# Six of sixteen modulation chunks multiplied and summed on VectorE, with TensorE adding the two sums over the partitions

## The chip, the cores and the metric

The kernel runs on one core of a Trainium2 chip. The metric is the device time of one execution, in microseconds. The kernel before took 989.61 us, the median of three runs (989.29, 989.61 and 990.34).

Five engines work side by side, each through its own instruction list in order, and meet only at semaphores: TensorE (PE) multiplies matrices, VectorE (DVE) and ScalarE (ACT) work elementwise, GpSimd (POOL) and SyncE (SP) mostly start DMA transfers here.

## The reference, cut to what matters

One layer of a diffusion backbone: an adaLN modulation, a bidirectional mLSTM, a pooling branch, a mixture of experts, a final norm. The change touches only the modulation, which is computed for two conditioning vectors, one for the 128 context tokens and one for the 512 latent tokens:

```python
mod_ctx = jax.nn.silu(c_ctx)[None, :] @ w_mod[l] + b_mod[l]      # (1, 6 * 1024)
mod_lat = jax.nn.silu(c) @ w_mod[l] + b_mod[l]                   # (1, 6 * 1024)
shift1, scale1, gate1, shift2, scale2, gate2 = [m[:, None, :] for m in jnp.split(mod, 6, axis=-1)]
h = _rmsnorm(x, g_norm1) * (1 + scale1) + shift1
proj = h @ w_in + b_in            # q, k, v, o, gates, pooling columns, branch gates
...
x = x + gate1 * (merged @ w_out)
h2 = _rmsnorm(x, g_norm2) * (1 + scale2) + shift2
```

`w_mod` is 1024 x 6144 in float32. The first 2048 columns (shift1, scale1) are needed before the input projection can start. The other 4096 (gate1, shift2, scale2, gate2) are needed much later.

## The kernel before, in words

**Weights come in chunks of 1 MB** (128 partitions x 2048 floats), from one array in the order of use, into four buffers `raw0` to `raw3`. SP's loop (line 411) takes chunk c into buffer c % 4 (in the stretch that matters here), and only when chunk c - 4 has been released (`raw_free`). It does so strictly in order: a chunk whose buffer is not free holds up all later ones.

**The stretch of the change** is the q/k projection, `for j in range(1, N_QK)` (line 1842), and the first value blocks behind it (line 1878). In step j, TensorE does two blocks of q or k columns (`block_q`, 48 matmuls of 128x320 each) and two modulation products (`mod2_product`, 2j-2 and 2j-1). Numbered as in SP's loop, the chunks are:

| step | q/k chunk multiplied | modulation chunks used (numbers 2j-2, 2j-1) | chunk split for the step after |
|---|---|---|---|
| j = 5 | 21 | 22, 23 (numbers 8, 9) | 24 |
| j = 6 | 24 | 25, 26 (10, 11) | 27 |
| j = 7 | 27 | 28, 29 (12, 13) | 30, the first value chunk |
| values | 30, 33, 34, 35 | 31, 32 (14, 15), behind the first value block | 33, 34, 35 |

**The split.** A float32 weight chunk that TensorE multiplies is first split in a high part (ScalarE, `split_hi`, line 631) and a low part (VectorE, `split_lo`, line 1024); three matmuls then make one product. `split_lo` releases the raw buffer. In step j, ScalarE waits until TensorE has finished step j-1, and for the chunk to have landed; VectorE's low part follows; TensorE needs both at step j+1.

**The modulation products** of the second part need no split. For 1024 = 8 x 128 rows and two halves of 2048 columns there are 16 chunks. `mod2_product` (line 1746) multiplies 128 rows of the 2048 columns by the 32-column tile `csil` (its first two columns are the two silu vectors, the rest is zero) in four matmuls, one for each 32-column strip of the array, and adds up eight chunks in PSUM bank 6. It releases the raw buffer. Once chunk 15 is in, ScalarE copies bank 6 (`mod_row2`, line 682), TensorE turns the row into columns (`mod2_turned`, line 1834), VectorE adds the bias (`mod_add`, line 1086), and TensorE transposes the result once more (line 1888). VectorE has little other work in steps 5 to 7: one `split_lo` each, and a small `mod_add(0)` in step 5.

**Value blocks.** `value_block(c, t)` (line 1853) is 12 matmuls of 128x512, for c = 0 to 3 and five token tiles t. Products 14 and 15 stand behind block (0, 0). Later on, PSUM results go to `Vt` with a bias. On GpSimd the ones column of `Vt` is set at the very start (line 477), and the first broadcast of the maxima (`load_maxima(0)`, line 484) waits for ScalarE's two row stores.

Of the kernel before, what the change touches and what calls it, by code (L numbers as in the profile page):

```python
# [16 lines left out]
ALU = mybir.AluOpType  # L17
# [3 lines left out]
P = 128  # L21
D = 1024
KT = D // P
# [14 lines left out]
CH = 2048  # L38
# [17 lines left out]
N_QK, N_MOD2, N_V, N_O, N_U, N_G, N_B, N_A, N_OUT = 8, 16, 4, 4, 2, 8, 2, 4, 4  # L56
# [6 lines left out]
AT_A = AT_B + N_B  # L63
AT_OUT = AT_A + N_A
N_DENSE = AT_OUT + N_OUT


C_ID, C_ONE, C_FWD, C_BWD, C_STRICT, C_IOTA, C_NEGF, C_NEGB = (P * i for i in range(8))
# [52 lines left out]
def qk_at(j):  # L121
    return AT_QK + 3 * (j - 1) if j else 0


def m2_at(g):
    return AT_QK + 1 + 3 * g if g < N_QK - 1 else AT_V - 1


def m2_chunk(i):
    return m2_at(i // 2) + i % 2  # L130


def v_at(i):
    return AT_V + i if i else AT_V - 2


def raw_slot(c):
    return (c - AT_O) % 2 if AT_O <= c < AT_G + 4 else c % NRAW


def raw_use(c):
    return sum(raw_slot(b) == raw_slot(c) for b in range(c))


def raw_uses(s):
    return sum(raw_slot(b) == s for b in range(N_DENSE))

# [5 lines left out]
def gate_up_at(p):  # L153
    return ECH * p - 2 if p else 0
# [6 lines left out]
def layer_kernel(nc, x_d, small_d, wst_d, wg_d, wpool_d, st_d, rcnt_d,  # L161
                 wexp_d, xt_d, gf_d, bv_d, y_d, so_d, mo_d):
    ctx = ExitStack()
    with ctx:
# [3 lines left out]
        def at(name, kib, shape, dt=F32):  # L168
            return nc.alloc_sbuf_tensor_at(name, shape, dt, offset=base + int(kib * 1024))

        def sem(name):
            return ctx.enter_context(nc.semaphore(name))
# [30 lines left out]
        raw = [at(f"raw{s}", 8 + 8 * s, [P, CH]) for s in range(NRAW)]  # L203
# [4 lines left out]
        hn = at("hn", 112, [P, KT, T])  # L208
# [12 lines left out]
        negM = at("negM", TMP + 22.5, [R16, T])  # L221

        QH, QL = whi, wlo
        csil = at("csil", 176.75, [P, KT, 32])
        vb = at("vb", 178.5, [P, D])
        mst = at("mst", 183, [P, 4, 2, KT])
# [92 lines left out]
        ps = ctx.enter_context(nc.psum_tensor("ps", [P, 8, 512], F32))  # L319
# [8 lines left out]
        def f32(t):  # L328
# [10 lines left out]
        raw_full = [sem(f"raw_full{s}") for s in range(NRAW)]  # L339
        raw_free = [sem(f"raw_free{s}") for s in range(NRAW)]  # L340
        hi_ready = sem("hi_ready")
        blk_ready, pair_free = sem("blk_ready"), [sem(f"pair_free{s}") for s in range(4)]
        o_hi, o_lo, s_sqh = sem("o_hi"), sem("o_lo"), sem("s_sqh")
        s_csil, s_sq, s_ssq, s_rstd, s_hn, s_hhi, s_hlo = (sem(n) for n in (
            "s_csil", "s_sq", "s_ssq", "s_rstd", "s_hn", "s_hhi", "s_hlo"))
        d_wg, s_gain = sem("d_wg"), sem("s_gain")
        s_wgh, s_wgl, s_gps, s_gate, s_lsg, s_grow, s_gtok = (sem(n) for n in (
            "s_wgh", "s_wgl", "s_gps", "s_gate", "s_lsg", "s_grow", "s_gtok"))
# [1 line left out]
        d_vb, d_rows = sem("d_vb"), sem("d_rows")  # L350
# [19 lines left out]
        f_a, f_b, f_c, f_y, f_sq, f_rs, f_out, s_out, s_sum1 = (sem(n) for n in (  # L370
            "f_a", "f_b", "f_c", "f_y", "f_sq", "f_rs", "f_out", "s_out", "s_sum1"))
# [11 lines left out]
        def chunk_used(eng, c):  # L383
            eng.wait_ge(raw_free[raw_slot(c)], raw_use(c) + 2)
# [88 lines left out]
        def _(gp):  # L473
            st = Steps(gp, g_steps)
            gp.memset(gOne[:, :], 1.0).then_inc(s_init, 1)

            gp.memset(Vt[:, :, :, DH:V1], 1.0).then_inc(s_init, 1)
            gp.wait_ge(d_rows, 32)
            chunk_used(gp, m2_at(N_QK - 1) + 1)

            def load_maxima(h):
                if h >= 2:
# [28 lines left out]
            for g, w in enumerate(WIN):  # L511
# [7 lines left out]
                n, s, src = GW + 2 * PAD, 1, 0  # L519
# [14 lines left out]
                else:  # L534
                    st.do(gp.tensor_copy(RP[0][:, w // 2:w // 2 + GR, :], xs))
                    n, s, src = GR + w - 1, 1, 0
# [13 lines left out]
                n, s, src = TC + 2 * PAD, 1, 0  # L550
# [71 lines left out]
        def _(act):  # L622
# [3 lines left out]
            st = Steps(act, a_steps)  # L626
# [18 lines left out]
            act.activation(wgh[:, :, :], wgr[:, :, :], ACT.Copy).then_inc(s_wgh, 1)  # L645
            act.preload_act_table_set(LN_EXP)
            split_hi(0, QH[0])
            act.wait_ge(s_ssq, 1)
            inv_rms(halves(rstd[:, :]), ps[:, 0:2, 0:HALF], D, s_rstd)
            for i in range(4):  # L650
                chunk_used(act, AT_M1 + 2 * i + 1)
# [28 lines left out]
                   .then_inc(q_free, 1)  # L680

            def mod_row2(i):
                chunk_used(act, m2_chunk(KT * i + KT - 1))
                if i:
                    act.wait_ge(s_modT, i + 4)
                act.activation(mrow[:, :], ps[:, 6, :], ACT.Copy).then_inc(s_mrow, 1)
# [141 lines left out]
            for j in range(N_G):  # L828
# [3 lines left out]
                for b in range(2):  # L832
                    f = 2 * j + b
# [10 lines left out]
            for j in range(N_A + 2):  # L844
                c = AT_A + j
# [76 lines left out]
            with act.Fori(0, last_round) as r:  # L922
# [43 lines left out]
                for p in range(NE):  # L966
                    c = gate_up_at(p) + 4
# [38 lines left out]
            for a in range(2):  # L1006
                n = slice(a * 512, a * 512 + 512)
# [9 lines left out]
        def _(dve):  # L1017
            st = Steps(dve, v_steps)

            def split_lo(c, hi, lo):  # L1020

                s = raw_slot(c)
                dve.wait_ge(hi_ready, split_no(c))
                dve.tensor_tensor(lo[:, :], raw[s][:, :], f32(hi[:, :]), ALU.subtract)\  # L1024
                   .then_inc(raw_free[s], 1)
# [60 lines left out]
            def mod_add(i):  # L1086
                dve.wait_ge(s_modT, i + 5)
                part = slice(16 + 16 * i, 32 + 16 * i)
                bias = col[:, B_MOD:B_MOD + 48][:, part].rearrange("p (g b) -> p b g", b=4)
                dve.tensor_tensor(mod[:, part, :].rearrange("p (g b) c -> p b g c", b=4),  # L1090
                                  ps[:, 7, 0:32].rearrange("p (b g c) -> p b g c", b=4, c=2),
                                  by(bias.unsqueeze(3), [P, 4, 4, 2]), ALU.add).then_inc(m_done, 1)

            def splits_lo(j):
                o = (j + 1) % 2
                split_lo(qk_at(j + 1) if j < N_QK - 1 else v_at(0), QH[o], QL[o])
                if j == 5:
                    mod_add(0)

            mf, mb = cst[0:R16, C_MF:C_MF + 1], cst[0:R16, C_MB:C_MB + 1]  # L1100
            segs = ((0, TC), (TC, T))
# [43 lines left out]
            def by_tile(a):  # L1145
# [5 lines left out]
                                    ALU.subtract))  # L1151
            dve.tensor_scalar(gF[:, 0:TC], gA[:, 0:TC], mlast[:, 0:1], None, ALU.subtract)\
               .then_inc(s_grow, 1)
            for j in range(4, N_QK):
                splits_lo(j)
            split_lo(AT_V + 1, QH[1], QL[1])
# [176 lines left out]
            for k in range(KT):  # L1333
# [9 lines left out]
                if k % 2 == 1:  # L1343
                    c = AT_A + 2 + k // 2
# [48 lines left out]
            last = NT - 1  # L1393
# [103 lines left out]
            with dve.Fori(0, last_round) as r:  # L1497
# [105 lines left out]
                for p in range(NE):  # L1603
                    c = gate_up_at(p) + 4
# [82 lines left out]
            for a in range(2):  # L1687
                n = slice(a * 512, a * 512 + 512)
# [4 lines left out]
        def _(pe):  # L1693
# [28 lines left out]
            def chunk_split(c):  # L1722
                pe.wait_ge(raw_free[raw_slot(c)], raw_use(c) + 2)
# [22 lines left out]
            def mod2_product(i):  # L1746
                c, k = m2_chunk(i), i % KT
                slot = raw_slot(c)
                pe.wait_ge(raw_full[slot], (raw_use(c) + 1) * 16)
                for g in range(4):  # L1750
                    last = nc.tensor.matmul(  # L1751
                        ps[32 * g:32 * g + 32, 6, :], csil[:, k, :], raw[slot][:, g * 512:(g + 1) * 512],
                        start=k == 0, stop=k == KT - 1, tile_position=(0, 32 * g))
                last.then_inc(raw_free[slot], 1)

            def mod_columns(rows, out):
                for b in range(4):
# [4 lines left out]
            def square_sums(sq, summed, done):  # L1762

                pe.wait_ge(summed, KT - 1)
                for a in range(2):
                    last = mm(ps[:, a, 0:HALF], ones, sq[:, 0, a * HALF:(a + 1) * HALF], True, True)
                last.then_inc(done, 1)
# [27 lines left out]
                mod_columns(mrow1[:, i % 2, :], ps[:, 5, 0:8])  # L1795

            pe.wait_ge(d_const, 16)
            square_sums(hn, s_sum1, s_ssq)
            pe.wait_ge(s_csil, 3)
            mod_pair(0)  # L1800
            mod_turned(0)
# [40 lines left out]
            for j in range(1, N_QK):  # L1842
                block_q(j, 0)
                if j == 1:
                    pe.wait_ge(s_gate, 2)
                elif j == 5:
                    mod2_turned(0)
                mod2_product(2 * j - 2)
                block_q(j, 1)
                pe.sem_inc(q_used, 1)  # L1850
                mod2_product(2 * j - 1)

            def value_block(c, t):
                u = c // 2 * NT + t
# [23 lines left out]
            for c in range(N_V):  # L1878
                for t in range(NT):
                    value_block(c, t)  # L1880
                    if c == 0 and t == 0:
                        mod2_product(N_MOD2 - 2)
                        mod2_product(N_MOD2 - 1)
                    if c == 0 and t == 2:
                        mod2_turned(1)
                    if c == 0 and t == 4:
                        pe.wait_ge(s_mst, 1)
                        nc.tensor.transpose(ps[0:64, 6, 0:P], mst[:, :, :, :].rearrange(
                            "p v c k -> p (v c k)"), ident).then_inc(s_mT, 1)
                    if c == 1 and t == 0:  # L1890
                        gate_rows()

            def score(h, i):
# [132 lines left out]
            for j in range(N_G):  # L2026
# [3 lines left out]
                for b in range(2):  # L2030
                    f = 2 * j + b
# [27 lines left out]
            for c in range(N_OUT):  # L2059
                chunk_split(AT_OUT + c)  # L2060
                for t in range(3 if c == 0 else 2):
                    if c == 0:
                        freed(pe, E_A + 4 + t)
                    for k in (2 * c, 2 * c + 1):
                        pe.wait_ge(s_mgl, k + 1)
                        last = out_pair(t, k, c)
# [33 lines left out]
            for k in range(2, KT):  # L2100
                last = out_pair(2, k, k // 2)
# [17 lines left out]
            last = NT - 1  # L2119
# [18 lines left out]
            for t in range(NT):  # L2138
                last = mm(out[:, t + 1:, :], ones_b[:, :], am[:, 0:NT - t, :], False, t == NT - 1)
# [6 lines left out]
            with pe.Fori(0, last_round) as r:  # L2146
# [61 lines left out]
                for table in range(2):  # L2208
                    for x in range(table + 1):
                        pe.wait_ge(s_oh, r * 4 + 2 * x + 1)  # L2210
                        for t in range(NT):
                            last = mm(ps[:, 4 + table, 0:2 * NE], onehot[:, x, t, :],
                                      pay[:, x, t, :, :].rearrange("p v e -> p (v e)"),
                                      x == 0 and t == 0, x == table and t == NT - 1)
# [22 lines left out]
            for t in range(NT):  # L2237
# [7 lines left out]
                for a in range(2):  # L2245
                    last = mm(ps[:, TAIL_BANK[t] + a, :], oh_T[:, t, :],
                              yb[(NE - 1) % 2][:, a * 512:(a + 1) * 512], False, True)
# [124 lines left out]
```

## Time and profile before

| | kernel before |
|---|---|
| median of 3 runs | 989.61 us |
| profiled execution, its own time | 987.24 us |
| its span, first to last instruction | 985.3 us |
| TensorE matmuls busy | 950.4 us (96%) |
| VectorE busy | 598.3 us (61%) |
| ScalarE busy | 475.9 us (48%) |
| mean granted TensorE clock | 0.99 |

All rows come from one profiled execution. Its own time is 2.37 us under the median of the plain runs. Times in rows are microseconds from the start of the span. In a timeline row "x8" is eight recorded instructions merged, the second number is how long they took together, and the brackets give the engine's idle time before it and what ended it. A float32 matmul of this kernel that is not split is recorded twice, so that x8 at line 1751 is one product of four matmuls.

### The profile page before, as it was taken

Reading aid. Unit: us, or ns where it says so; the run is one execution under the profiler, and the core shown is the slowest. Engines: PE = TensorE matmul, PEld = TensorE weight load, DVE = VectorE, ACT = ScalarE, POOL = GpSimd, SP = SyncE. Lnnn points to the kernel's source line nnn. Section 1 sums busy time; section 2 is a strip of 40 time slices with the busy share of each in tenths; the row PEclk is TensorE's granted clock in tenths of the full one; section 3 lists DMA queues with packets and bytes.
Section 4 is the critical chain, followed back from the end, with each engine's and each line's share of the span. In section 5 each row is a group of like instructions: output and inputs, shape, how many; then the busy total and the mean of one; then the engine's idle time right before and its main releaser. Section 6 shows DMA issues by size and latency. Waiting matters only on the chain.

```text
span 985.3 us, 13948 instructions
## 1 busy us (share of the span) xinstructions
PE 950.4 (96%) x5636; PEld 839.1 (85%) x5636; DVE 598.3 (61%) x763; ACT 475.9 (48%) x638; POOL 123.4 (13%) x133
## 2 busy tenths in 40 slices
PE   3999999999999999999999999989999999999986
PEld 1788888789999999999999998877888888888862
DVE  5353311234788862321344555449999999999998
ACT  5552121223566643122341242255878787787863
POOL 0000000001110009970000000002012111111100
PEclk9999999999999999999999999989999999999998
DMA  9735454613434163233212218148999999999974
GB/s 376 298 134 212 171 214 171 263 68 90 130 95 111 65 225 128 86 123 124 65 65 86 86 49 336 59 155 313 421 421 409 423 419 416 419 413 408 398 278 168
DMA packets 36192, 219.02 MB, mean 222 GB/s; under 512 B 3968, under 2 KB 4160, under 8 KB 15648
## 3 DMA queue, kind: packets, MB, share of 16 engines
q1 hardware_dynamic: 26496, 180.25, 46.6%
q0 software_dynamic: 8768, 35.15, 10.4%
q10 hardware_dynamic: 864, 2.73, 0.7%
q8 instruction: 45, 0.74, 0.3%
q14 instruction: 19, 0.16, 0.0%
HBM read 200.70 MB, written 17.42 MB: 221 GB/s over the span
## 4 chain that ended last, share of the span: by engine, by line
PE 91%; DVE 4%; DMA 3%; ACT 1%; issue 1%; SPq 0%; DVEq 0%; POOLq 0%; ACTq 0%
PE ps L1695 85%; PE ps L1751 2%; PE ps L2159 1%; DMA xT<-in_x 1%; PE ps L2187 1%; DMA raw<-in_wst 1%; PE ps L1740 0%; DMA xg<-h2scr,slot_rows 0%; PE ps L2010 0%; PE ps L1903 0%; DVE rowA L1650 0%; DVE xr L1653 0%; DVE xr L1657 0%; PE ps L2082 0%; DMA rowB<-yscr 0%
## 5 line engine op out<-in xcount | busy, mean ns | idle before, releaser
L1024 DVE TENSOR_TENSOR wlo<-raw,whi 128x2048 fp32r<-128x2048 f32 x29 | 66.7, 2301 | 158.3 <-ACT whi L631 158.3
L1695 PE MATMUL ps<-hhi,whi 128*128 128x320 f32 x672 | 155.8, 313 | 0.0
L1695 PE MATMUL ps<-hlo,whi 128*128 128x320 f32 x672 | 153.4, 309 | 0.0
L1695 PE MATMUL ps<-hhi,wlo 128*128 128x320 f32 x672 | 153.4, 309 | 0.0
L1695 PEld LDWEIGHTS ps<-hhi,whi 128*128 128x128 f32 x672 | 112.2, 189 | 11.3 <-ACT QK L678 5.9
L1695 PEld LDWEIGHTS ps<-hlo,whi 128*128 128x128 f32 x672 | 112.6, 188 | 0.0
L1695 PEld LDWEIGHTS ps<-hhi,wlo 128*128 128x128 f32 x672 | 112.6, 188 | 0.0
L631 ACT ACTIVATE whi<-raw 128x2048 fp32r<-128x2048 f32 x29 | 55.4, 1911 | 103.3 <-PE ps L1695 62.5
L1506 DVE TENSOR_TENSOR olo<-raw,ohi 128x2048 fp32r<-128x2048 f32 x32 | 72.4, 2288 | 3.8 <-ACT ohi L928 3.8
L1506 DVE TENSOR_TENSOR wlo<-raw,whi 128x2048 fp32r<-128x2048 f32 x31 | 70.3, 2289 | 5.2 <-ACT whi L928 4.7
L928 ACT ACTIVATE whi<-raw 128x2048 fp32r<-128x2048 f32 x32 | 61.3, 1917 | 18.8 <-PE ps L1695 18.8
L928 ACT ACTIVATE ohi<-raw 128x2048 fp32r<-128x2048 f32 x32 | 61.2, 1917 | 18.0 <-PE ps L1695 18.0
L835 ACT ACTIVATE TH<-ps,small 128x640 f32<-128x640 f32 x16 | 12.7, 795 | 88.6 <-PE ps L1695 88.6
L1695 PE MATMUL ps<-whi,xgh 128*128 128x512 f32 x128 | 50.8, 397 | 0.3 <-DVE xgl L1582 0.2
L1695 PE MATMUL ps<-ohi,xgh 128*128 128x512 f32 x128 | 50.7, 396 | 0.0
L1695 PE MATMUL ps<-whi,xgl 128*128 128x512 f32 x128 | 50.0, 391 | 0.0
L1695 PE MATMUL ps<-ohi,xgl 128*128 128x512 f32 x128 | 50.0, 390 | 0.0
L1695 PE MATMUL ps<-wlo,xgh 128*128 128x512 f32 x128 | 49.9, 390 | 0.0
L1695 PE MATMUL ps<-olo,xgh 128*128 128x512 f32 x128 | 49.8, 389 | 0.0
L1695 PE MATMUL ps<-hhi,owh 128*128 128x320 f32 x160 | 49.3, 324 | 0.1
L1695 PE MATMUL ps<-hhi,owl 128*128 128x320 f32 x160 | 46.9, 309 | 0.0
L1695 PE MATMUL ps<-hlo,owh 128*128 128x320 f32 x160 | 46.8, 309 | 0.0
(372 smaller groups left out, 1995.7 us busy)
## 6 DMA issues: line engine op xcount, KB each, us to landing
raw<-in_wexp SPq DMA_DIRECT2D x64, 1024.0 KB, 8.8
raw<-in_wst SPq DMA_DIRECT2D x60, 1024.0 KB, 5.2
eraw<-in_wexp SPq DMA_DIRECT2D x32, 1024.0 KB, 8.5
nm<-negscr POOLq DMA_DIRECT2D x8, 640.0 KB, 7.2
wib<-wiscr POOLq DMA_DIRECT2D x8, 512.0 KB, 6.2
xT<-in_x SPq DMA_DIRECT2D x4, 640.0 KB, 7.0
yscr<-zeros POOLq DMA_DIRECT2D x1, 2560.0 KB, 12.8
xr<-in_xt SPq DMA_DIRECT2D x1, 2560.0 KB, 9.9
```

The lines of the kernel that those rows point to most:

```text
L631: act.activation(dst[:, :], raw[raw_slot(c)][:, :], ACT.Copy).then_inc(hi_ready, 1)
L835: act.activation(halves(TH[:, gate_at(f), :]), pair(E_TH[f]), ACT.Tanh, scale=0.5, bias=col[:, 36 + f:37 + f]).then_inc(pair_free[E_TH[f] ...
L928: act.activation(ehi[i % ESPL][:, :], eraw[s][:, :], ACT.Copy).then_inc(e_hi, 1)
L1024: dve.tensor_tensor(lo[:, :], raw[s][:, :], f32(hi[:, :]), ALU.subtract)\
L1506: dve.tensor_tensor(elo[i % ESPL][:, :], eraw[s][:, :], f32(ehi[i % ESPL][:, :]), ALU.subtract).then_inc(e_free[s], 1)
L1695: return nc.tensor.matmul(out, lhsT, rhs, start=start, stop=stop)
L1751: last = nc.tensor.matmul(ps[32 * g:32 * g + 32, 6, :], csil[:, k, :], raw[slot][:, g * 512:(g + 1) * 512], start=k == 0, stop=k == KT - 1 ...
L2159: last = nc.tensor.transpose(ps[:, 6 + k // 4, (k % 4) * P:(k % 4 + 1) * P], xg[b][:, k * P:(k + 1) * P], ident)
L2187: last = nc.tensor.transpose(ps[:, 2 * (p % 2), f * P:(f + 1) * P], act_[:, f * P:(f + 1) * P], ident)
```

## The change

Modulation chunks 8 to 13 are no longer multiplied on TensorE. VectorE multiplies each with the two silu values of its partition (a per-partition scalar for each conditioning vector) and adds it into two 128x2048 tiles, `acc0` and `acc1`: two instructions for each chunk, 12 in all, set into `splits_lo` behind the low split of that step. `raw_free` of these six chunks is now released by VectorE. On TensorE, `mod2_summed` then adds both tiles over the partitions into bank 6, with a tile `take` that is 1 in one column: two groups of four matmuls, behind value block (0, 1). The turn of the row moves from behind block (0, 2) to behind (0, 3), the transpose from (0, 4) to (1, 0), the gate rows from (1, 0) to (1, 1). `acc` lies where `Vt` comes later, so GpSimd's memset of the ones column moves behind its waits, in front of the first `load_maxima`.

```diff
+M2_SUM = range(8, 14)
...
+        acc = [at(f"acc{x}", 152 + 8 * x, [P, CH]) for x in range(2)]
+        take = at("take", 173, [P, 2, 32])
...
+            gp.wait_ge(d_rows, 32)
+            gp.wait_ge(s_ssq_m2, 2)
+            chunk_used(gp, m2_at(N_QK - 1) + 1)
             gp.memset(Vt[:, :, :, DH:V1], 1.0).then_inc(s_init, 1)
-            gp.wait_ge(d_rows, 32)
-            chunk_used(gp, m2_at(N_QK - 1) + 1)
...
             def mod_row2(i):
-                chunk_used(act, m2_chunk(KT * i + KT - 1))
+                if i:
+                    act.wait_ge(s_ssq_m2, 2)
+                else:
+                    chunk_used(act, m2_chunk(KT - 1))
...
+            def mod_sum(i):
+                c, k = m2_chunk(i), i % KT
+                slot = raw_slot(c)
+                dve.wait_ge(raw_full[slot], (raw_use(c) + 1) * 16)
+                if i == M2_SUM[0]:
+                    st.on(dve.tensor_scalar(acc[0][:, :], raw[slot][:, :], csil[:, k, 0:1], None, ALU.mult))
+                    dve.tensor_scalar(acc[1][:, :], raw[slot][:, :], csil[:, k, 1:2], None, ALU.mult)\
+                       .then_inc(raw_free[slot], 1)
+                    return
+                before = m2_chunk(i - 1)
+                st.wait()
+                dve.wait_ge(raw_free[raw_slot(before)], raw_use(before) + 2)
+                st.on(dve.scalar_tensor_tensor(acc[0][:, :], raw[slot][:, :], csil[:, k, 0:1], acc[0][:, :],
+                                               ALU.mult, ALU.add))
+                dve.scalar_tensor_tensor(acc[1][:, :], raw[slot][:, :], csil[:, k, 1:2], acc[1][:, :],
+                                         ALU.mult, ALU.add).then_inc(raw_free[slot], 1)
+
             def splits_lo(j):
                 o = (j + 1) % 2
                 split_lo(qk_at(j + 1) if j < N_QK - 1 else v_at(0), QH[o], QL[o])
+                if 2 * j - 2 in M2_SUM:
+                    mod_sum(2 * j - 2)
                 if j == 5:
                     mod_add(0)
+                if 2 * j - 1 in M2_SUM:
+                    mod_sum(2 * j - 1)
...
+            def mod2_summed():
+                chunk_split(m2_chunk(M2_SUM[-1]))
+                for x in range(2):
+                    for g in range(4):
+                        last = nc.tensor.matmul(
+                            ps[32 * g:32 * g + 32, 6, :], take[:, x, :], acc[x][:, g * 512:(g + 1) * 512],
+                            start=False, stop=x == 1, tile_position=(0, 32 * g))
+                last.then_inc(s_ssq_m2, 1)
...
-                mod2_product(2 * j - 2)
+                if 2 * j - 2 not in M2_SUM:
+                    mod2_product(2 * j - 2)
                 block_q(j, 1)
                 pe.sem_inc(q_used, 1)
-                mod2_product(2 * j - 1)
+                if 2 * j - 1 not in M2_SUM:
+                    mod2_product(2 * j - 1)
...
                     if c == 0 and t == 0:
                         mod2_product(N_MOD2 - 2)
                         mod2_product(N_MOD2 - 1)
-                    if c == 0 and t == 2:
+                    if c == 0 and t == 1:
+                        mod2_summed()
+                    if c == 0 and t == 3:
                         mod2_turned(1)
-                    if c == 0 and t == 4:
+                    if c == 1 and t == 0:
                         pe.wait_ge(s_mst, 1)
...
-                    if c == 1 and t == 0:
+                    if c == 1 and t == 1:
                         gate_rows()
```

On VectorE, in steps 5 to 7 and up to the split of chunk 33, the kernel before has this (`raw_68` to `raw_71` are the buffers raw0 to raw3, so chunk c is in `raw_(68 + c % 4)`):

```order
L1024 TENSOR_TENSOR wlo_74<-raw_68,whi_72 128x2048
L1090 TENSOR_TENSOR mod<-ps,small 128x4x4x2
L1024 TENSOR_TENSOR wlo_75<-raw_71,whi_73 128x2048
L1024 TENSOR_TENSOR wlo_74<-raw_70,whi_72 128x2048
L1024 TENSOR_TENSOR wlo_75<-raw_69,whi_73 128x2048
```

The same place on VectorE in the changed kernel (`acc_95` and `acc_96` are the two sums):

```order
L1106 TENSOR_SCALAR acc_95<-raw_70,csil 128x2048
L1107 TENSOR_SCALAR acc_96<-raw_70,csil 128x2048
L1097 TENSOR_TENSOR mod<-ps,small 128x4x4x2
L1113 SCALAR_TENSOR_TENSOR acc_95<-raw_71,csil,acc_95 128x2048
L1115 SCALAR_TENSOR_TENSOR acc_96<-raw_71,csil,acc_96 128x2048
L1031 TENSOR_TENSOR wlo_75<-raw_71,whi_73 128x2048
L1113 SCALAR_TENSOR_TENSOR acc_95<-raw_69,csil,acc_95 128x2048
L1115 SCALAR_TENSOR_TENSOR acc_96<-raw_69,csil,acc_96 128x2048
L1113 SCALAR_TENSOR_TENSOR acc_95<-raw_70,csil,acc_95 128x2048
L1115 SCALAR_TENSOR_TENSOR acc_96<-raw_70,csil,acc_96 128x2048
L1031 TENSOR_TENSOR wlo_74<-raw_70,whi_72 128x2048
L1113 SCALAR_TENSOR_TENSOR acc_95<-raw_68,csil,acc_95 128x2048
```

Between two low splits VectorE now has four full-width instructions, and both `acc` rows of a chunk have to end before its buffer is loaded again. The last row begins number 12, in `raw0`: the buffer that chunk 32 goes to.

On TensorE, from the end of step 7 to value block (0, 1), the kernel before has these rows (the rows of a value block repeat, so that one or two stand for it):

```order
L1751 MATMUL ps<-raw_69,csil 32x512 x4
L1695 MATMUL ps<-whi_72,hhi 128x512
...
L1695 MATMUL ps<-whi_72,hlo 128x512
L1751 MATMUL ps<-raw_71,csil 32x512 x4
L1751 MATMUL ps<-raw_68,csil 32x512 x4
L1695 MATMUL ps<-whi_72,hhi 128x512
```

And these in the changed kernel:

```order
L1726 MATMUL ps<-whi_72,hlo 128x512
L1782 MATMUL ps<-raw_71,csil 32x512 x4
L1782 MATMUL ps<-raw_68,csil 32x512 x4
L1726 MATMUL ps<-whi_72,hhi 128x512
...
L1791 MATMUL ps<-acc_95,take 32x512 x4
L1791 MATMUL ps<-acc_96,take 32x512 x4
```

The product in front of the value block is gone, products 14 and 15 stand where they stood, and the two groups on `acc` come twelve matmuls behind them.

## Rows read from the trace of the kernel before

**Rows 1.** The page: shares of the chain that ended last, by engine.

```profile
PE 91%; DVE 4%; DMA 3%; ACT 1%; issue 1%; SPq 0%; DVEq 0%; POOLq 0%; ACTq 0%
```

**Rows 2.** Critical chain, 164 to 190 us: start, duration, engine and line, instructions.

```profile
164.11 7.23 PE ps L1695 x48
171.34 0.99 PE ps L1751 x8
172.33 2.95 PE ps L1695 x12
175.28 1.85 PE ps L1751 x16
177.14 12.11 PE ps L1695 x56
```

**Rows 3.** Windows: length, busy us (count) of each engine, granted clock, DMA share, GB/s.

```profile
192.00:232.00 40.00, 40.00 (x191) 33.36 (x191) 15.07 (x16) 7.55 (x17) 0.59 (x1) 1.00 0.15 53
```

**Rows 4.** Timeline of ScalarE, evictions of blocks with no product between them.

```profile
384.63 0.79 ACT L835 ACTIVATE TH<-ps,small 128x640 f32<-128x640 f32 x1 [3.14 <-PE ps L1695]
391.67 0.79 ACT L835 ACTIVATE TH<-ps,small 128x640 f32<-128x640 f32 x1 [6.25 <-PE ps L1695]
```

**Rows 5.** Timeline of VectorE, evictions of value blocks with nothing between them.

```profile
201.56 0.69 DVE L1172 TENSOR_TENSOR Vt<-ps,vb 128x512 f32<-128x512 f32 x1 [2.03 <-PE ps L1695]
204.28 0.69 DVE L1172 TENSOR_TENSOR Vt<-ps,vb 128x512 f32<-128x512 f32 x1 [2.03 <-PE ps L1695]
```

**Rows 6.** VectorE groups by form: form and count, busy us, mean ns, idle before.

```profile
L1376 DVE SCALAR_TENSOR_TENSOR ht<-xr,ss,g 128x1024 f32<-128x1024 f32 x4 | 5.1, 1280 | 3.6 <-ACT ss L636 3.6
L1419 DVE SCALAR_TENSOR_TENSOR ht<-ht,ss,s 128x512 f32<-128x512 f32 x2 | 1.4, 750 | 0.6 <-ACT ss L908 0.6
```

**Rows 7.** Timeline of VectorE, one and two tensor operands on 640 elements.

```profile
98.44 0.53 DVE L1115 TENSOR_SCALAR gB<-gB,small 16x640 f32<-16x640 f32 x1
99.01 0.87 DVE L1116 SCALAR_TENSOR_TENSOR gB<-gC,small,gB 16x640 f32<-16x640 f32 x1
```

**Rows 8.** Timeline of SP: issues of chunks 27, 30 and 32.

```profile
139.49 0.33 SPq L416 DMA_DIRECT2D raw<-in_wst  x1
155.94 0.33 SPq L416 DMA_DIRECT2D raw<-in_wst  x1
164.17 0.33 SPq L416 DMA_DIRECT2D raw<-in_wst  x1
```

**Rows 9.** Line 416, the issue of chunk 32 alone: from issue to landing.

```profile
DMA to landing us min/median/max: 5.1/5.1/5.1
```

**Rows 10.** Timelines of ScalarE and VectorE: splits of chunks 24 and 27.

```profile
129.22 2.29 DVE L1024 TENSOR_TENSOR wlo<-raw,whi 128x2048 fp32r<-128x2048 f32 x1 [14.07 <-ACT whi L631]
131.43 0.18 DVE L1090 TENSOR_TENSOR mod<-ps,small 128x32 f32<-128x32 f32 x1
...
144.54 1.92 ACT L631 ACTIVATE whi<-raw 128x2048 fp32r<-128x2048 f32 x1 [5.28 <-DMA raw<-in_wst]
...
146.49 2.29 DVE L1024 TENSOR_TENSOR wlo<-raw,whi 128x2048 fp32r<-128x2048 f32 x1 [14.88 <-ACT whi L631]
```

**Rows 11.** Windows around two stretches at a lower clock, columns as in rows 3.

```profile
19.50:25.40 5.90, 3.17 (x24) 1.16 (x20) 4.56 (x8) 3.13 (x6) 0.00 (x0) 1.00 1.00 407
25.40:31.00 5.60, 5.53 (x30) 4.39 (x30) 1.09 (x2) 1.76 (x3) 0.00 (x0) 0.70 1.01 424
27.00:29.00 2.00, 2.00 (x9) 1.79 (x8) 0.52 (x1) 0.20 (x1) 0.00 (x0) 0.50 1.01 422
650.00:659.00 9.00, 9.00 (x43) 7.99 (x43) 3.36 (x18) 7.61 (x6) 0.00 (x0) 0.62 0.80 287
```

**Rows 12.** Timeline of TensorE, the last wait ahead of the first of them.

```profile
25.47 1.06 PE L1740 MATMUL ps<-raw,csil 128*32 128x512 f32 x8 [2.07 <-DMA raw<-in_wst]
```

**Rows 13.** Timelines of GpSimd and VectorE: the first broadcast, and its first reader.

```profile
186.85 0.92 POOL L484 DMA_DIRECT2D nm<-negscr  x1 [185.38 <-DMA wiscr<-gI]
210.83 1.55 DVE L1184 TENSOR_TENSOR nmd<-nm,small 128x640 f32<-128x640 f32 x2
```

More of the change, by code:

```diff
@@ L343, in layer_kernel @@
         o_hi, o_lo, s_sqh = sem("o_hi"), sem("o_lo"), sem("s_sqh")
-        s_csil, s_sq, s_ssq, s_rstd, s_hn, s_hhi, s_hlo = (sem(n) for n in (
-            "s_csil", "s_sq", "s_ssq", "s_rstd", "s_hn", "s_hhi", "s_hlo"))
+        s_csil, s_sq, s_ssq_m2, s_rstd, s_hn, s_hhi, s_hlo = (sem(n) for n in (
+            "s_csil", "s_sq", "s_ssq_m2", "s_rstd", "s_hn", "s_hhi", "s_hlo"))
         d_wg, s_gain = sem("d_wg"), sem("s_gain")
@@ L647, in _ @@
             split_hi(0, QH[0])
-            act.wait_ge(s_ssq, 1)
+            act.wait_ge(s_ssq_m2, 1)
             inv_rms(halves(rstd[:, :]), ps[:, 0:2, 0:HALF], D, s_rstd)
@@ L1153, in _ @@
                .then_inc(s_grow, 1)
+            st.do(dve.memset(take[:, :, :], 0.0))
+            for x in range(2):
+                st.on(dve.memset(take[:, x, x:x + 1], 1.0))
             for j in range(4, N_QK):
@@ L1752, in mod2_product @@
                         ps[32 * g:32 * g + 32, 6, :], csil[:, k, :], raw[slot][:, g * 512:(g + 1) * 512],
-                        start=k == 0, stop=k == KT - 1, tile_position=(0, 32 * g))
+                        start=i in (0, M2_SUM[-1] + 1), stop=i == KT - 1, tile_position=(0, 32 * g))
                 last.then_inc(raw_free[slot], 1)
+            def mod2_summed():
+                chunk_split(m2_chunk(M2_SUM[-1]))
+                for x in range(2):
+                    for g in range(4):
[3 more added lines that the diff above has]
+                last.then_inc(s_ssq_m2, 1)
             def mod_columns(rows, out):
@@ L1797, in _ @@
             pe.wait_ge(d_const, 16)
-            square_sums(hn, s_sum1, s_ssq)
+            square_sums(hn, s_sum1, s_ssq_m2)
             pe.wait_ge(s_csil, 3)
```

## The prediction

> **What bounds the kernel now.** I read the page first: the chain that ended last is 91% TensorE [rows 1]. So I took that chain piece by piece around the change, and it is TensorE alone there: 48 matmuls of a block, the eight records of a product, the next block, and no wait between them [rows 2]. In the value blocks behind, TensorE is busy 40.00 us of 40 [rows 3]. Whatever TensorE is spared or made to wait here moves all that follows, since every later load and eviction hangs on its progress. The other views are for the question whether VectorE and the loads can keep up: timelines of VectorE, ScalarE and SP give the durations of the loop that feeds TensorE.
>
> **What is taken off TensorE.** A block with the product behind it lasts from 164.11 to 172.33, 8.22 us [rows 2]. The same 48 matmuls without a product come every 391.67 - 384.63 = 7.04 us [rows 4]. So a product costs 1.18 us. Number 8 stands behind the turn of the first row, not behind a block, and I count 1.0 us for it, the duration of its own piece. Six products: 5 x 1.18 + 1.0 = 6.9 us.
>
> **What is added on TensorE.** Two groups of four matmuls of 128x512, of the same shape as products 14 and 15. Block (0, 0) and these two last from 172.33 to 177.14, 4.81 us; a value block alone comes every 204.28 - 201.56 = 2.72 us [rows 2, 5]. That is 2.1 us for the two groups. Turn, transpose and gate rows only change places: nothing. TensorE alone would gain 6.9 - 2.1 = 4.8 us.
>
> **What VectorE has to do for it.** No row has these instructions at 2048 elements, so I take them from shorter ones. Two tensor operands and a scalar: 0.750 us at 512 and 1.280 us at 1024 [rows 6], 1.035 ns an element, 2.34 us at 2048. An instruction that waits for nothing starts some 0.08 us before the end of the one ahead (131.43 after 129.22 + 2.29) [rows 10], a dependent one 0.04 us behind it (99.01 after 98.97) [rows 7]. A chunk's two instructions: 2.26 + 2.34 + 0.04 = 4.64 us. The first chunk has one tensor operand: 0.53 us at 640 elements against 0.87 [rows 7], about half the price for each element with 0.2 us fixed, so 1.27 us at 2048 and 2.5 us for the pair. The bounds are 1.2 and 2.3 us an instruction in both cases; for the later chunks I stay at 2.34, since all rows with two tensor operands lie on that slope, and for the first pair at 2.5.
>
> The Trainium skill ("VectorE: DVE Perf Modes", the perf-mode tier table) lists float32 `tensor_scalar` at double rate, 1227 ns for 2048 elements, and `tensor_tensor` at single rate, 2293 ns. It has no row for the form that multiplies and adds; if that went at double rate, the sum would be that of the first rival below. The 0.87 us row of this trace speaks against it.
>
> **The loop that this makes.** It is what the change costs, and the diff does not show it. The raw buffers go round: chunk 27 is loaded when 23 is released, 30 when 26, 32 when 28. TensorE released 23, 26 and 28; now VectorE does, in its own order, behind the low split of the step and behind the earlier sums. In time order, from the low split of chunk 24, which starts at 129.22 as before [rows 10]:
>
> - Number 8 from 131.43 to 133.9; the small bias add; number 9 ends at 138.7 and releases chunk 23.
> - SP issues chunk 27 at 138.8 (139.49 before [rows 8]). From that issue to ScalarE's split it took 144.54 - 139.49 = 5.05 us, and from there to VectorE's 1.95 [rows 8, 10]. So the low split of 27 starts at 145.8. TensorE wants it at about 151.3: in time.
> - Next instruction 2.21 us later, at 148.0: number 10 to 152.65, number 11 to 157.25. SP issues chunk 30, the first value chunk, at 157.35, not 155.94 [rows 8]. High split at 162.4, low split 164.35 to 166.64.
> - TensorE gets to value block (0, 0) at 172.33 - 6.9 = 165.4 and waits until 166.7: 1.3 us.
> - Number 12 from 166.56 to 171.2 releases chunk 28. Only then can SP load chunk 32, number 15: at 171.3, where it was 164.17 [rows 8]. It landed 5.1 us after its issue [rows 9]: TensorE can begin product 15 at 176.35.
> - TensorE would come to product 15 one block and one product after 165.4, at 165.4 + 2.95 + 0.93 = 169.3 [rows 2]. The two waits make 176.35 - 169.3 = 7.05 us together: 1.3 in front of block (0, 0) and 5.75 in front of product 15.
> - Number 13 ends at 175.8, TensorE is at `mod2_summed` at about 180: no wait. Chunk 33 is issued at 175.9, split by 185.3, wanted past 190: no wait.
>
> The sum on TensorE: -6.9 + 2.1 + 7.05 = +2.25, and 0.05 because product 15 no longer runs into the tail of 14: +2.3 us.
>
> **The clock.** A wait of 5.75 us in front of product 15 is longer than any in the stretch now. In the window 19.5 to 25.4 TensorE was busy 3.17 us of 5.90, with 2.07 us of waiting at its end [rows 11, 12]; behind it the granted clock was 0.50, the lower of its two levels (1.2 of 2.4 GHz), and over 25.4 to 31 its mean was 0.70. At 5.60 x 0.30 that cost 1.7 us. The other slow stretch of the trace, 650 to 659 behind a thin run of small matmuls, has a mean of 0.62: 9.0 x 0.38 = 3.4 us [rows 11]. I expect the fall here, and take 1.7 us, the nearer case; bounds 0 and 3.4. The Trainium skill ("TensorE: Matmul & The Clock Gate", What's actually happening) says that the throttled state is the default and activity lifts it; by that too the idle stretch ends at the lower level, and this trace agrees (0.50).
>
> **Moved and hidden edits.** The row copy on ScalarE now waits for `mod2_summed`, and behind it stand the two row stores, the copy of the transposed row and the split of chunk 34. That split is wanted only at block (2, 0), 10 us behind the gate rows. On GpSimd the ones memset and the first broadcast wait for the stores; the broadcast was issued at 186.85 and first read at 210.83 [rows 13], 24 us of cover against a shift of some 8 us. If that cover were gone, each microsecond would count once. The memsets of `take` fall into VectorE's idle time (14.07 us before the low split [rows 10]).
>
> **Total.** 2.3 + 1.7 = +4.0 us. On the profiled execution's own 987.24 that makes 991.2. The plain runs have a median of 989.61, 2.4 us above it, so the time to compare is 993.6.
>
> **Rivals.**
>
> - VectorE is fast enough, and the gain stays. The price is 989.61 - 4.8 = 984.8. The two waits shrink by four times what a pair gets shorter (numbers 9 to 12 are in the chain). At 4.64 us they are 7.05 us; the change pays once they are under 4.8, a pair under 4.08 us. At double rate (2.5 us a pair) they are gone. Against it: 1.035 ns an element. Chance 0.07.
> - The same waits, but the clock holds, because the product in front and the block behind are dense: +2.3, 991.9. For it: the clock stood at 1.00 over all 40 us of value blocks [rows 3]. Against it: a 2.07 us wait was enough at 25.4. Chance 0.14.
> - The first pair at single rate as well (2.3 us an instruction, 4.6 for 2.5): the whole loop is 2.1 us later, all of it in the waits: +6.1, 995.7. Against it the 0.53 us row. Chance 0.08. A slow stretch like that of 650 to 659 would give +5.7, 995.3; it is part of the forecast's own spread.
> - The delay is taken up later, by a wait that is there anyway: no change. Against it: TensorE has no wait in the value blocks [rows 3], and what waits for data later waits for something TensorE started. Chance 0.05.
>
> **How the numbers follow.** The forecast has 0.66. Measurement of this kernel can tell about 0.2% from no change, 2.0 us. The forecast and the slower first pair are slower: 0.74. Of the clock-holds case at +2.3, so near the border, I give two thirds to slower and the rest to no change: slower 0.83. No change: 0.05 + 0.05 = 0.10. Faster 0.07. The range runs from 991.2, a little under the clock-holds case, to 996.6, with the slow first pair or the long slow stretch and a bit more for slopes that are off: a pair 0.1 us longer adds 0.4 us.
>
> **What would show it.** In the changed profile: products at the old line fall from 128 records to 80, and blocks in steps 5 to 7 come every 7.04 us. The multiply-and-add instructions last 2.34 us, the first two 1.27. SP's issues of chunks 30 and 32 come at 157.3 and 171.3. TensorE waits 1.3 us in front of the first value block for the low split, and 5.75 us in front of product 15 for a load; behind it the granted clock is 0.50 for some 3 us. Block (1, 0) starts about 4 us later than 177.14 + 12.11 = 189.3 [rows 2], and the distance stays the same to the end. I would be wrong if the form runs at double rate, if chunk 32 is issued before 164.2, or if the 4 us are not there at the end of the span.

## The result, and the profile after

| | before | changed |
|---|---|---|
| median, 7 runs each on the same chip | 989.28 us | 992.5 us |
| lowest and highest | 987.29, 990.34 | 991.04, 993.86 |
| ratio of the runs, 95% interval | | 1.0039 (1.003 to 1.0049) |
| span of the profiled execution | 985.3 us | 989.2 us |
| VectorE busy | 598.3 us | 623.3 us |

The changed kernel is slower by 3.9 us by the ratio, with an interval of 3.0 to 4.8 us. The forecast was 4.0 us (993.6 us on the earlier median of 989.61): 2.3 us by late loads, with what TensorE is spared already taken off, and 1.7 us by the clock.

VectorE's timeline in steps 5 to 7 of the changed kernel (start, duration, engine and line, operation, count, idle time before it):

```profile
127.10 2.29 DVE L1031 TENSOR_TENSOR wlo<-raw,whi 128x2048 fp32r<-128x2048 f32 x1 [14.13 <-ACT whi L635]
129.31 1.28 DVE L1106 TENSOR_SCALAR acc<-raw,csil 128x2048 f32<-128x2048 f32 x1
130.50 1.28 DVE L1107 TENSOR_SCALAR acc<-raw,csil 128x2048 f32<-128x2048 f32 x1
131.70 0.19 DVE L1097 TENSOR_TENSOR mod<-ps,small 128x32 f32<-128x32 f32 x1
131.91 2.35 DVE L1113 SCALAR_TENSOR_TENSOR acc<-raw,csil,acc 128x2048 f32<-128x2048 f32 x1
134.19 2.34 DVE L1115 SCALAR_TENSOR_TENSOR acc<-raw,csil,acc 128x2048 f32<-128x2048 f32 x1
143.76 2.29 DVE L1031 TENSOR_TENSOR wlo<-raw,whi 128x2048 fp32r<-128x2048 f32 x1 [7.23 <-ACT whi L635]
...
162.33 2.29 DVE L1031 TENSOR_TENSOR wlo<-raw,whi 128x2048 fp32r<-128x2048 f32 x1 [7.01 <-ACT whi L635]
```

The instructions last what the forecast had from shorter ones in [rows 6, 7]: 2.35 us for 2.34, 1.28 for 1.27. Between two low splits VectorE has some 7 us of idle time that this order does not use: it waits for the split, and the sums stand behind it.

The chain that ended last shows the loop itself (start, duration, what), where [rows 2] had TensorE alone:

```profile
120.18 4.88 DMA raw<-in_wst
...
136.56 5.17 DMA raw<-in_wst
...
150.71 2.35 DVE acc L1113
153.06 2.27 DVE acc L1115
155.33 0.02 issue
155.35 4.95 DMA raw<-in_wst
...
160.38 1.92 ACT whi L635
...
164.54 2.35 DVE acc L1113
166.88 2.28 DVE acc L1115
169.16 0.02 issue
169.18 4.94 DMA raw<-in_wst
174.12 0.04 issue
174.16 1.93 PE ps L1782 x8
176.09 4.47 PE ps L1726 x12
180.56 1.85 PE ps L1791 x16
```

Read it from the end. Product 15 (line 1782, at 174.16) waited for the load issued at 169.18; that waited for number 12 on VectorE; that stood behind the low split of the first value chunk, whose load was issued at 155.35, when number 11 ended. From 120 to 174 the chain is not on TensorE.

TensorE's timeline has the two waits:

```profile
164.68 0.50 PE L1726 MATMUL ps<-whi,hhi 128*128 128x512 f32 x1 [1.24 <-DVE wlo L1031]
167.59 1.06 PE L1782 MATMUL ps<-raw,csil 128*32 128x512 f32 x8
174.16 1.93 PE L1782 MATMUL ps<-raw,csil 128*32 128x512 f32 x8 [5.50 <-DMA raw<-in_wst]
```

And the windows behind them show the clock (length, busy us and count of PE, PEld, DVE, ACT, POOL, granted clock, DMA share, GB/s), as [rows 11] did for another stretch:

```profile
170.00:173.00 3.00, 0.00 (x0) 0.00 (x0) 3.00 (x2) 0.00 (x0) 0.00 (x0) 0.91 0.92 317
173.00:179.00 6.00, 4.84 (x15) 2.60 (x16) 0.90 (x1) 0.09 (x1) 0.00 (x0) 0.50 0.71 258
179.00:184.00 5.00, 5.00 (x29) 2.71 (x29) 2.29 (x1) 2.93 (x3) 0.00 (x0) 0.97 1.02 428
192.00:232.00 40.00, 40.00 (x188) 32.92 (x188) 14.46 (x15) 9.53 (x18) 0.59 (x1) 1.00 0.19 65
```

After the idle stretch the clock is at 0.50, the lower of its two levels (1.2 GHz). Product 15 and the value block behind it last 1.93 and 4.47 us. Behind them TensorE is busy without a gap, as in [rows 3]. GpSimd's first broadcast moved as well, with its memset of 0.21 us in front:

```profile
189.37 0.21 POOL L483 MEMSET Vt<- 128x40 f32 x1 [188.01 <-DMA wiscr<-gI]
189.44 0.92 POOL L488 DMA_DIRECT2D nm<-negscr  x1
```

It was first read at 213.33, so this cover held.

**A distance inside the trace.** Single executions differ in their first 45 us, between 617 and 951 us and in their last 35, by up to 3.5 us in each (last section). So I compare a distance that leaves these out, and call it local: from SP's issue of chunk 24 to ScalarE's first copy of the gate rows. Before, it is 193.18 - 122.24 = 70.94 us, and 73.66 with the one value block (2.72 us, [rows 5]) that now stands in front of the gate rows. In the changed kernel it is 198.39 - 120.18 = 78.21 us: 4.55 us more. The two ends, first before, then in the changed kernel (each issue row has two issues merged, and the time is that of the first):

```profile
122.24 0.81 SPq L416 DMA_DIRECT2D raw<-in_wst  x2
193.18 0.24 ACT L712 ACTIVATE a_tok<-ps 128x80 f32<-128x80 f32 x1 [0.97 <-PE ps L1874]
...
120.18 0.81 SPq L419 DMA_DIRECT2D raw<-in_wst  x2
198.39 0.24 ACT L719 ACTIVATE a_tok<-ps 128x80 f32<-128x80 f32 x1 [0.94 <-PE ps L1916]
```

### The profile page after: what moved, and what is told of

It is laid out like the page before. It is cut to its first block, busy times and chain, and to the rows that moved or that the text cites. A ratio compares the mean times of both kernels' runs of the same rounds, so it can differ in the third digit from the quotient of the medians.

```text
span 989.2 us, 13904 instructions
## 1 busy us (share of the span) xinstructions
PE 949.4 (96%) x5604; PEld 838.5 (85%) x5604; DVE 623.3 (63%) x778; ACT 475.8 (48%) x638; POOL 123.8 (13%) x133
## 4 chain that ended last, share of the span: by engine, by line
PE 85%; DVE 6%; DMA 5%; ACT 2%; issue 1%; SPq 0%; DVEq 0%; POOLq 0%; ACTq 0%
PE ps L1726 80%; DMA raw<-in_wst 3%; PE ps L2203 1%; PE ps L1782 1%; DVE acc L1113 1%; DVE acc L1115 1%; DMA xT<-in_x 1%; ACT whi L635 1%; PE ps L2231 1%; PE ps L1771 1%; DVE wlo L1031 0%; DMA xg<-h2scr,slot_rows 0%; PE ps L2054 0%; PE ps L1947 0%; DVE rowA L1681 0%
```

## The experiments

All runs are compared with the kernel before, several times in turn on the same chip. "Local" is the distance just described, less 73.66 us. The last column is the ratio times 989 us.

| run | expected | local | ratio (95%) | in us |
|---|---|---|---|---|
| changed kernel | +4.0 | +4.55 | 1.0039 (1.003 to 1.0049) | +3.9 |
| sums one step earlier | -4.8 | -4.95 | 0.9948 (0.9928 to 0.9967) | -5.1 |
| four sums | -2.4 | -2.56 | 0.9965 (0.9951 to 0.9979) | -3.5 |
| filler in the wait | +1.5 | +1.47 | 1.0016 (1.0006 to 1.0027) | +1.6 |
| width 1536 | -2.7 | -3.01 | 0.9966 (0.9952 to 0.9981) | -3.4 |
| product 15 later | -3.5 | -3.97 | 0.9953 (0.9938 to 0.9968) | -4.6 |
| all eight, earlier | -6.7 | -7.04 | 0.9924 (0.9911 to 0.9937) | -7.5 |

**The same work one step earlier.** Number 8 to 11 in step 5, 12 and 13 in step 6:

```diff
                 split_lo(qk_at(j + 1) if j < N_QK - 1 else v_at(0), QH[o], QL[o])
-                if 2 * j - 2 in M2_SUM:
-                    mod_sum(2 * j - 2)
                 if j == 5:
+                    mod_sum(8)
                     mod_add(0)
-                if 2 * j - 1 in M2_SUM:
-                    mod_sum(2 * j - 1)
+                    for i in (9, 10, 11):
+                        mod_sum(i)
+                elif j == 6:
+                    for i in (12, 13):
+                        mod_sum(i)
```

> The changed kernel with the same twelve VectorE instructions, but each pair of sums one step earlier: numbers 8, 9, 10, 11 in step 5 and 12, 13 in step 6, where VectorE was idle. Theory A (VectorE releases the raw buffers too late because its sums stand behind the low split of the step, so the loads of chunks 30 and 32 come late; and the wait in front of product 15 lowers TensorE's clock): chunk 30 is issued at about 146 and 32 at about 153, both waits vanish, the clock stays at 1.00 there, and only TensorE's saving is left: 4.8 us less than before, about 984.5, ratio 0.995. Rival B (25 us more of VectorE work, or the new places in the value blocks, cost time whatever the order): it stays at about 3.5 us above before, 993, ratio 1.0035.

984.7 us against 988.2, ratio 0.9948. The same twelve instructions, 5.1 us less than before in place of 3.9 more. SP issued chunk 30 at 147.44 and chunk 32 at 154.17. TensorE's window from 60 to 200 us shows no wait, and the clock stays up:

```profile
60.00:200.00 140.00, 140.00 (x899) 122.77 (x899) 63.80 (x64) 32.01 (x32) 1.58 (x3) 1.00 0.52 194
```

VectorE was busy for longer than before here and it cost nothing. This is the run that rules out a price for the VectorE work as such.

**Only four chunks on VectorE.**

```diff
-M2_SUM = range(8, 14)
+M2_SUM = range(8, 12)
```

> The changed kernel with only numbers 8 to 11 summed on VectorE; 12 and 13 are products on TensorE again, which then releases chunk 28 as before. Theory A: chunk 30 still waits for VectorE's number 11 (issued at about 155.3 on the time scale of the changed kernel's trace), but TensorE has 2.4 us more to do before the first value block, so its 1.3 us wait is gone, and product 15 does not wait. TensorE saves 4 products (4.5 us) and pays 2.1: 2.4 us less than before, 986.9, ratio 0.9976. Rival B (VectorE work as such): two thirds of the loss stay, about 2.4 us above before, 991.7.

985.21 us against 988.2, ratio 0.9965. With number 12 back on TensorE, chunk 32 was issued at 160.72, right after that product, and landed before TensorE came to it. Number 13 is a product again too, and 14 and 15 ran in one piece (TensorE's timeline):

```profile
167.82 1.07 PE L1782 MATMUL ps<-raw,csil 128*32 128x512 f32 x8
171.77 1.92 PE L1782 MATMUL ps<-raw,csil 128*32 128x512 f32 x16
```

So the last two of the six chunks turn the change from a gain to a loss.

**Filler matmuls in the wait.** This one is for the clock alone: the waits stay, and TensorE is kept busy in the longer one.

```diff
                         mod2_product(N_MOD2 - 2)
+                        keep_busy(12)
                         mod2_product(N_MOD2 - 1)
```

> The changed kernel with 12 extra matmuls of 128x256 (a result that nobody reads) between products 14 and 15, in the wait for chunk 32. Theory A: they take about 5.2 us of the 5.5 us wait, so that they delay nothing, and the granted clock stays at 1.00 behind it: product 15 lasts 1.06 us instead of 1.93 and value block (0, 1) 2.95 instead of 4.47, 2.4 us less than the changed kernel: about 1.5 us above before, 990.8, ratio 1.0015. Rival: the lower clock costs nothing in the end, or filler matmuls cost their own time: as the changed kernel (992.5) or up to 5 us more.

990.49 us against 988.2, ratio 1.0016. The interval 1.0006 to 1.0027 lies below the changed kernel's 1.003 to 1.0049. The filler took the place of the wait, and product 15 and the block behind it ran at full clock:

```profile
165.71 0.50 PE L1726 MATMUL ps<-whi,hhi 128*128 128x512 f32 x1 [0.61 <-DVE wlo L1031]
...
169.63 5.45 PE L1726 MATMUL ps<-small 128*128 128x256 f32 x24
175.06 1.06 PE L1782 MATMUL ps<-raw,csil 128*32 128x512 f32 x8
176.06 0.50 PE L1726 MATMUL ps<-whi,hhi 128*128 128x512 f32 x1
...
179.00 1.50 PE L1791 MATMUL ps<-acc,take 128*32 128x512 f32 x12
```

From the start of product 15 to the sum over the partitions it is 179.00 - 175.06 = 3.94 us. In the changed kernel it is 180.56 - 174.16 = 6.40 us. So the lower clock cost 2.5 us. The filler did not delay product 15: it started 4.85 us after the issue of its load (170.21), for 4.98 us in the changed kernel.

**Shorter sums.** VectorE's instructions cover 1536 of 2048 columns; the last 512 of both sums are set to zero ahead and left out of the result. The first pair (`tensor_scalar`) is cut to 1536 in the same way.

```diff
...
-                st.on(dve.scalar_tensor_tensor(acc[0][:, :], raw[slot][:, :], csil[:, k, 0:1], acc[0][:, :],
-                                               ALU.mult, ALU.add))
+                st.on(dve.scalar_tensor_tensor(acc[0][:, 0:1536], raw[slot][:, 0:1536], csil[:, k, 0:1],
+                                               acc[0][:, 0:1536], ALU.mult, ALU.add))
...
+            for x in range(2):
+                st.on(dve.memset(acc[x][:, 1536:], 0.0))
```

> The changed kernel with VectorE's twelve instructions on 1536 of the 2048 columns; the last 512 columns of both sums are set to zero early and left out of the result. Nothing else differs. Theory A: a pair takes 3.56 us instead of 4.62, the loop up to the load of chunk 32 is 4.9 us shorter, the wait in front of the first value block is gone and 2.1 us are left of that in front of product 15; with the clock at 1.00 it is 2.7 us below before, 986.6, ratio 0.9973; if the clock still falls, 1 us below. Slope: four times what a pair gets shorter. Rival B (a cost for the instructions as such, a quarter less of them): a quarter of the loss goes, 991.6.

985.09 us against 988.2, ratio 0.9966. The instructions lasted 1.81 us, chunk 32 was issued at 165.56 (the span's start is another one here: chunk 24 was issued at 121.84), and of the 1.24 and 5.50 us of waiting in the changed kernel this was left, with the clock at 1.00 behind it (2.1 us expected):

```profile
170.56 1.06 PE L1785 MATMUL ps<-raw,csil 128*32 128x512 f32 x8 [1.73 <-DMA raw<-in_wst]
```

A quarter off each sum took 5.0 us of 6.74 off the waits. That is the lever of a loop: four pairs that get 1.08 us shorter each, and 0.5 us from the first one. A price for each instruction would have given back a quarter.

**The reader later.** VectorE and the loads as in the changed kernel; TensorE comes to product 15 two value blocks later.

```diff
                         mod2_product(N_MOD2 - 2)
+                    if c == 0 and t == 2:
                         mod2_product(N_MOD2 - 1)
-                    if c == 0 and t == 1:
                         mod2_summed()
-                    if c == 0 and t == 3:
+                    if c == 0 and t == 4:
                         mod2_turned(1)
```

> The changed kernel with VectorE's order as it is; on TensorE product 15 and the sum over the partitions stand behind value block (0, 2), and the turn of the row behind (0, 4). Theory A: the load of chunk 32 is as late as before (issued at about 169), but three value blocks and product 14 stand in front of its reader, 1.0 + 3 x 2.9 us from 164.7, so it lands as TensorE comes to it. The 5.5 us wait and the lower clock go, the 1.2 us wait in front of block (0, 0) stays: 4.8 - 1.3 = 3.5 us below before, ratio 0.9965. Rival (late loads matter elsewhere too, for the split of chunk 33, or ScalarE's copy of the row behind it): less than half of that.

982.52 us against 987.53, ratio 0.9953. Chunk 32 was issued at 168.48, as late as ever, but no wait stands in front of product 15 now. Of the two waits one is left:

```profile
163.98 0.50 PE L1726 MATMUL ps<-whi,hhi 128*128 128x512 f32 x1 [0.79 <-DVE wlo L1031]
```

It is 0.79 us where 1.2 were expected, which is most of the 0.5 us by which the local gain is larger than forecast. The run also tells that the late loads behind it did no harm: TensorE has no wait from 165 to 200 us.

**All eight chunks, with the earlier order.** Numbers 14 and 15 are summed on VectorE too, behind the low split of the first value chunk.

```diff
-M2_SUM = range(8, 14)
+M2_SUM = range(8, 16)
...
             for j in range(4, N_QK):
                 splits_lo(j)
+            mod_sum(14)
+            mod_sum(15)
             split_lo(AT_V + 1, QH[1], QL[1])
...
-                    if c == 0 and t == 0:
-                        mod2_product(N_MOD2 - 2)
-                        mod2_product(N_MOD2 - 1)
-                    if c == 0 and t == 1:
+                    if c == 0 and t == 2:
                         mod2_summed()
-                    if c == 0 and t == 3:
+                    if c == 0 and t == 4:
                         mod2_turned(1)
```

> The order of the run with sums one step earlier, and numbers 14 and 15 also multiplied and summed on VectorE, behind the low split of the first value chunk; TensorE adds both sums behind value block (0, 2), and turns the row behind (0, 4). Theory A (only late loads cost anything): number 14 and 15 end about 168, before TensorE is through block (0, 2) at about 170, and nothing waits. TensorE saves two more products, 1.9 us (1.85 in the chain before): 6.7 us below before, ratio 0.9932, 2 us below the run with six sums earlier. Rival: behind the first value block the loads of chunks 33 to 35 wait for VectorE in turn, or the split of 33 comes late for block (1, 0): the gain stays at 4.8 us or less.

980.44 us against 987.53, ratio 0.9924: the fastest version, 7.5 us below the kernel before. Its last sum ended at 170.3, TensorE began to add at 172.85, and this stretch too is without a wait:

```profile
60.00:200.00 140.00, 140.00 (x893) 124.14 (x892) 74.41 (x69) 34.10 (x34) 1.57 (x3) 1.00 0.53 194
```

Against the run with six sums earlier it is 2.1 us less in the local distance, for two products at 1.9 us together. The two ratios come from separate sets of runs and their intervals overlap, so the local distance is what tells them apart.

## Why the prediction was right

- **TensorE's own saving, 4.8 us.** Shown by the run with the sums earlier: same edits on TensorE, nothing waiting, -4.95 us local.
- **VectorE's prices.** 2.34 us forecast, 2.35 measured; 1.27 and 1.28. The trace agrees with the Trainium skill ("VectorE: DVE Perf Modes", the perf-mode tier table) on `tensor_scalar` in float32 (1227 ns there, 1.28 us here), and adds the form with a multiply and an add: at 2.35 us it runs at the rate of the low split with its two tensor operands (2.29 us).
- **The loop.** It is the step on which the sign depends, and it came out link by link. With the trace's start 2.06 us earlier (chunk 24 at 120.18 for 122.24), chunk 30 was forecast at 155.3 and came at 155.35, chunk 32 at 169.2 and came at 169.18. The waits were forecast at 1.3 and 5.75 us and are 1.24 and 5.50. The low splits on the way were in time, as forecast.
- **The clock.** That it falls was right; 1.7 us was too little. Measured are 2.5 us, between the stretch that I took and the 3.4 us of the other one [rows 11]. The forecast had the lower clock for some 3 us; it lasted 5.0, from 174.16 until the matmul at 179.18 got shorter. In the stretch of 1.7 us TensorE was busy for 3.17 of the 5.90 us ahead, and the product at 25.47 still ran at full clock, 1.06 us [rows 11, 12]; here it did nothing for 5.50 us, and product 15 already started at the lower clock. I had the nearest row by length, not by how idle TensorE was. That this is what made the price larger is my reading, and no run varied it. Nor was the 2.07 us wait all that it hung on at 25.4, as the prediction has it: in the changed kernel's execution the clock was down there by 22.11 (a product of 1.83 us), behind waits of 0.44 and 0.72 us. Together: 1.24 + 5.50 + 2.5 - 4.8 = +4.4 us, for 4.55 measured locally. The mechanism was right; the sum had 0.3 us too much for the waits and 0.8 us too little for the clock, which partly cancel. That the whole runs then gave +3.9 beside a forecast of +4.0 is closer than these errors allow, and luck.
- **The rivals.** VectorE at double rate is out by its durations. "The clock holds" is out by the window at 0.50; its price was near, +2.3 forecast and +1.47 local with the filler, or 2.1 with the 0.6 us by which the wait in front of the value block was shorter there. The slow first pair is out (1.28 us). That a later wait takes up the delay is out too: TensorE has no gap in the 40 us behind, and the runs as a whole move as the local distance does, each within its interval.
- **Hidden edits.** The moved turn, transpose, gate rows, memset and broadcast cost nothing that a row shows: the run with the sums earlier has them all, and no wait.

What stays open: in six of the seven comparisons the whole time is 0.2 to 0.9 us lower than the local distance would have it. About 0.2 us of it stands in the traces. The kernel before has a wait of 0.27 us on TensorE (at 344.09, for VectorE's `DG`) that the changed kernel does not have, and from the issue of chunk 24 to ScalarE's copy into `h2T` at 616.98 us (619.29 in the changed kernel) the difference is 4.37 us where the local one is 4.55; the other six are 0.2 to 0.3 us lower there too. The rest is within the interval of each ratio, and no run here was made to tell whether it is more than noise.

## What to carry to other kernels

When work moves from the bounding engine to one with idle time, ask what it hands back when it is done. Here it was a load buffer, and the new owner gave it back behind an instruction that itself waited for an earlier load, so that 18.6 us of VectorE, DMA and ScalarE stood against the 14.1 us (two blocks at 7.04) in which TensorE now did a step. The same twelve instructions, put into the idle time ahead of that instruction, turned +3.9 us into -5.1 us.

## What I had not expected of the hardware

The first 45 us scatter between executions: chunk 24 was issued between 119.94 and 123.45 us in the eight profiled executions. Both of these are from variants of the changed kernel (product 15 later, and four sums) that do not differ in that stretch. In the two traces that I compared, one load on the chain, issued at 18.7 in both, landed in 6.73 us before and 5.55 after, and the product behind it lasted 1.06 us [rows 12] before and 1.72 after, already at the lower clock. Between 617 and 951 us, where there are more stretches at the lower clock, the same work took 333.8 to 337.0 us. The tail scatters too. Four matmuls on the last rows lasted 1.98 us before,

```profile
958.74 1.98 PE L1695 MATMUL ps<-rowB,small 128*128 128x512 f32 x4 [2.00 <-DMA rowB<-yscr]
```

and 3.68 us in the changed kernel, behind a wait of nearly the same length:

```profile
960.92 3.68 PE L1726 MATMUL ps<-rowB,small 128*128 128x512 f32 x4 [2.12 <-DMA rowB<-yscr]
```

So a wait of 2 us can leave the clock up in one execution and have it down in the next. In all eight executions this wait was 1.93 to 2.12 us long. In five the four matmuls lasted 1.98 us; in three they lasted 2.76, 3.27 and 3.68 us, and the shortest wait (1.93) is among these three. The three places together moved a span, against what the local distance tells, by up to 3.8 us from that of the kernel before (the run with the sums earlier), as much as the change itself: the difference of two spans would have been a poor measure of it.
